# A two-block transformer on one core: 32x32 transposes and small transfers in place of 64 TensorE transposes, and four steps at new places

## The chip, the cores and the metric

One core of a Trainium2 chip runs the whole program. The metric is the device time of one execution in microseconds; lower is better. Before the change it is 789.58 us, the median of 3 runs (789.48 to 789.94). The core has TensorE (PE), VectorE (DVE), ScalarE (ACT), GpSimd (POOL) and SyncE (SP, which only issues transfers); each works through its own list in order, and semaphores tie the lists together.

## The reference, cut to what matters

One sequence of 256 positions and 1024 features goes through two blocks, all in float32.

```python
# first block
h = rmsnorm(x, norm1_g);  u = h @ w_in                       # 7168 columns: x_rnn g_rnn q k v g_br
ya = rg_lru(causal_dwconv(x_rnn)) * gelu(g_rnn)              # a linear recurrence over positions
q, k = rmsnorm per head(q, k)                                # 8 heads of 128
yb = causal softmax attention(q, k, v)                       # one block of 256 keys
x = x + (sig(g0) * (ya @ w_proj_rnn) + sig(g1) * (yb @ w_proj_attn)) @ w_out
h = rmsnorm(x);  x = x + (gelu(causal_dwconv(h @ w_up)) * (h @ w_gate)) @ w_down
# second block
h = rmsnorm(x);  proj = h @ w_in_2
o_a = windowed attention with sinks (8 heads of 64);  o_b = latent attention (8 heads, 64 + 32)
x = x + (sig(g_a) * (o_a @ w_o_swa) + sig(g_b) * (o_b @ w_o_mla)) @ w_out_2
h = rmsnorm(x);  x = x + (silu(h @ w_gate_2) * (h @ w_up_2)) @ w_down_2     # the last FFN
return rmsnorm(x, final_norm_g)
```

## The kernel before, in words

**Slabs.** All weights lie in HBM as 132 slabs of 128 x 2048 float32 (1 MB), in the order of their use (`slab_plan`, L47). SyncE loads slab s into one of three buffers `raw` as soon as VectorE is done with slab s - 3 (`load`, L476). ScalarE rounds it to a high part `whi` (L547), VectorE subtracts to get the low part `wlo` (L1010, `pre(s)`), and TensorE adds up three products for each pair of tiles (high by high, high by low, low by high; L1630, L1633, L1634, or L1677 and L1679). Activations are split in the same way. ScalarE may overwrite `whi` of slab s - 3 only when TensorE is done with it.

**Order.** Every engine's list is written out over the same slab numbers. The numbers that matter here: q, k and v are slabs 9 to 20, the gates of the first block 21 to 28 (`S_GATE` = 21), the two branch products 29 to 36, `w_out` 37 to 40, the first FFN 41 to 73, the second block up to 98, the last FFN 99 to 131. The FFNs are loops of three slabs a pass on each engine.

**Attention of the first block** (`att(step)` on ScalarE L574, VectorE L1057, TensorE L1721). One head enters at each slab from 21 on, and its stages lie one slab apart: at step u TensorE turns q and k of head u against an identity matrix (four transposes, L1731) and ScalarE copies them out of PSUM (L581, L582); at step u + 1 come the scores (L1742, L1743) and VectorE's mask and maximum; at u + 2 ScalarE's exponential; at u + 3 VectorE's normalisation (L1061 to L1063); at u + 4 TensorE turns the three tiles of probabilities (L1751) and ScalarE copies them to `pT` (L588); at u + 5 TensorE multiplies by the values (L1759, L1761) and both parts of the result are made (L592, L1075). The branch product from slab 33 on waits for these parts, head by head. Where q and k come from: ScalarE evacuates their slabs to `q_s` and `k_s` with positions on the partitions; VectorE scales k in the slab-18 turn of its list (L1235), which TensorE's first transposes wait for.

**The row sums.** TensorE sums squares of x for the first normalisation (`sums(0)`, L1707) between two chunks k of slab 2 (`hook` at L1950, before chunk 4), then ScalarE takes a root (L572) and VectorE the reciprocal.

**Second block.** Pairs of heads go through a similar pipeline (`PAIR_*`, L216 to L220; `pair_hi`, `pair_lo`, `pair_norm`). `pair_values` puts pairs p and p + 1 in one PSUM bank; `pair_lo` and `pair_norm` are called in that order in VectorE's list (L1480). `turned_lo` and `pre` of slab 96 (L1516) come at the start of `w_out`.

**The last FFN** (`ffn`, on SP L489, ACT L810, DVE L1321, PE L2045). In pass j TensorE makes the up and gate products of tile j + 1 and then the down product of tile j. The down product adds up in four PSUM banks over all passes. Ahead of the first one, `turned()` (L2049) puts the residual X, turned by sixteen transposes, into those banks. VectorE's `post(j)` sums and scales the products and makes the low parts of the next slabs between its steps.

```python
# L2098, TensorE in the first pass
if first and which == 2:
    e.wait_ge(rms_root, ROOTS[n])
    turned()
down(j - 1, s + 2, (base + 4) % RING, first=first and which == 1)
```

Of the kernel before, what the change touches and what calls it, by code (L numbers as in the profile page):

```python
# [16 lines left out]
P = 128  # L17
SEQ = 256
# [189 lines left out]
LAG_S, LAG_E, LAG_N, LAG_PT, LAG_PV = 1, 2, 3, 4, 5  # L208
# [40 lines left out]
def program(nc, t):  # L249
    f32, f32r = mybir.dt.float32, mybir.dt.float32r  # L250
    ALU, ACT, AX = mybir.AluOpType, mybir.ActivationFunctionType, mybir.AxisListType.X
    with ExitStack() as ctx:
# [71 lines left out]

        rnn_t = pr[:, :, :].rearrange("p a n -> p (a n)")[:, 0:4 * SEQ].rearrange("p (a n) -> p a n", a=4)
# [32 lines left out]
        PST, PSS, PSPT, PSPV, PSA, PSB = ps[2], (ps[3], ps[7]), (ps[4], ps[6]), ps[5], ps[6], ps[7]  # L358
# [28 lines left out]
        pair_pT = pT, VV[:, 1280:2048].rearrange("p (u n) -> p u n", u=2)  # L387
        PSX = (ps[0], ps[1], ps[2], ps[3])
# [27 lines left out]
        qk_ss, qk_scaled, v_ready = sem("qk_ss"), sem("qk_scaled"), sem("v_ready")  # L416
        aT, aTe, aS, aM, aE, aN, aPT, aPTe, aPV, aH, aL = (sem(n) for n in (
# [55 lines left out]
        def _(sp_eng):  # L473
# [14 lines left out]

            def ffn(base, then=None):  # L489
# [23 lines left out]
            for s in range(2 * RING, FFN1):  # L513
                load(s)
            ffn(FFN1)
# [17 lines left out]
        def _(e):  # L533
# [40 lines left out]
            def att(step):  # L574
                u = unit_of(step)
                if u is not None:
                    b = u % 2
                    e.wait_ge(aT, u + 1)
                    if u >= 2:
                        e.wait_ge(aS, u - 1)  # L580
                    e.activation(qT[:, b, :], PST[:, 0:SEQ], ACT.Copy)  # L581
                    e.activation(kT[:, b, :], PST[:, SEQ:2 * SEQ], ACT.Copy, scale=qkg[:, :]).then_inc(aTe, 1)  # L582
                u = unit_of(step - LAG_PT)
                if u is not None:
                    e.wait_ge(aPT, u + 1)
                    if u >= 2:
                        e.wait_ge(aPV, u - 1)
                    e.activation(pT[:, u % 2, :], PSPT[u % 2][:, 0:3 * P], ACT.Copy).then_inc(aPTe, 1)  # L588
# [5 lines left out]
                if u is not None:  # L594
                    e.wait_ge(aM, u + 1)
                    if u >= 3:
                        e.wait_ge(aPT, u - 2)
# [6 lines left out]
            def pair_turned(p):  # L604

                e.wait_ge(aT, pair(p))
# [22 lines left out]
            def pair_probs(p):  # L629

                e.wait_ge(aPT, pair(p))
# [3 lines left out]
            def pair_hi(p):  # L635

                e.wait_ge(aPV, pair(p + 1))
                e.activation(pairs[2][0][:, p:p + 2, :], PSPV2[p], ACT.Copy).then_inc(aH, 2)
# [360 lines left out]
        def _(e):  # L999
# [16 lines left out]

            def bc2(ap, n):
# [1224 lines left out]
```

## Time and profile before

| what | value |
|---|---|
| median of 3 runs | 789.58 us (789.48 to 789.94) |
| the profiled execution, its own time | 789.17 us |
| its span, first to last instruction | 787.4 us |
| instructions | 11265 |
| VectorE busy | 591.8 us (75%) |
| ScalarE busy | 452.6 us (57%) |
| moved by DMA | 141.08 MB, mean 179 GB/s |
| granted TensorE clock over the span | 0.999 of full speed |

A row of the timeline gives the start (us from the span's start), the duration of a group of like instructions, the engine, the line of the kernel, the operation, what it writes and reads, the shape, the count, and in brackets how long the engine was idle before it and on whose work. Matmuls overlap: a duration on PE reaches beyond the start of the next one, so the distance of two starts is what an instruction takes of the engine's time. A float32 product of the attention shows as two instructions (x2 where the source has one). "SPq" is SyncE issuing a transfer, not the transfer itself.

### The profile page before, as it was taken

The numbers are of one execution on the slowest core, as the hardware profiler recorded it, in microseconds if no ns is written. First come the engines' busy times: TensorE is split into PE (matmuls) and PEld (weight loads), VectorE is DVE, ScalarE is ACT, GpSimd is POOL, SyncE is SP. The second block draws the span as 40 slices with busy tenths as digits, with TensorE's granted clock in tenths as the row PEclk, the third lists the DMA queues.
The fourth block names the chain that finished last, engine by engine and source line by source line (L and its number), as shares of the span: only waits on it lengthen the run. The fifth ranks groups of instructions, "written<-read, shape, count | busy, mean of one in ns | idle before, by whom it ended". The sixth has DMA issues, their size and how long they took to land.

```text
span 787.4 us, 11265 instructions
## 1 busy us (share of the span) xinstructions
PE 780.1 (99%) x4246; PEld 669.1 (85%) x4246; DVE 591.8 (75%) x727; ACT 452.6 (57%) x591; POOL 44.3 (6%) x63
## 2 busy tenths in 40 slices
PE   9999999999999999999999999999999999999997
PEld 9998888888888888888888897888788888888886
DVE  6986897566578998778887867777789666666664
ACT  7679765666345654544444758765556535454444
POOL 0220231000000000000000031220000000000000
PEclk9999999999999999999999999999999999999999
DMA  8745555443545455465454352544445645454521
GB/s 329 246 171 198 193 185 214 158 160 122 199 161 199 148 207 196 171 209 205 167 206 160 144 219 106 173 163 159 161 143 206 214 163 210 161 212 171 202 107 53
DMA packets 22100, 141.08 MB, mean 179 GB/s; under 512 B 3410, under 2 KB 3762, under 8 KB 6066
## 3 DMA queue, kind: packets, MB, share of 16 engines
q1 hardware_dynamic: 21682, 140.13, 49.5%
q10 hardware_dynamic: 384, 0.49, 0.2%
q8 instruction: 22, 0.36, 0.2%
q14 instruction: 12, 0.10, 0.0%
HBM read 139.33 MB, written 1.05 MB: 178 GB/s over the span
## 4 chain that ended last, share of the span: by engine, by line
PE 96%; ACT 1%; DMA 1%; DVE 1%; issue 0%; SPq 0%
PE pp L1677 24%; PE pp L1630 18%; PE pp L1634 18%; PE pp L1633 18%; PE pp L1679 12%; PE pp L1819 1%; DMA first<-in_first 1%; PE pp L1851 1%; PE pp L1831 1%; PE pp L1894 0%; PE pp L1731 0%; PE pp L1743 0%; PE pp L1759 0%; ACT whi L657 0%; PE pp L1751 0%
## 5 line engine op out<-in xcount | busy, mean ns | idle before, releaser
L1010 DVE TENSOR_TENSOR wlo<-raw,whi 128x2048 fp32r<-128x2048 f32 x129 | 296.3, 2298 | 82.6 <-ACT whi L547 82.2
L547 ACT ACTIVATE whi<-raw 128x2048 fp32r<-128x2048 f32 x129 | 246.4, 1911 | 99.1 <-PE pp L1634 82.3
L1677 PE MATMUL pp<-ahilo,whi 128*128 128x512 f32 x832 | 261.9, 396 | 0.1
L1679 PEld LDWEIGHTS pp<-ahilo,wlo 128*128 128x128 f32 x832 | 156.3, 188 | 36.7
L1679 PE MATMUL pp<-ahilo,wlo 128*128 128x256 f32 x832 | 163.5, 278 | 0.0
L1630 PE MATMUL pp<-whi,ahilo 128*128 128x512 f32 (+1 forms) x336 | 133.1, 396 | 0.6 <-ACT first L778 0.6
L1634 PE MATMUL pp<-whi,ahilo 128*128 128x512 f32 (+1 forms) x336 | 130.5, 388 | 0.0
L1633 PE MATMUL pp<-wlo,ahilo 128*128 128x512 f32 (+1 forms) x336 | 130.3, 388 | 0.0
L1677 PEld LDWEIGHTS pp<-ahilo,whi 128*128 128x128 f32 x832 | 128.3, 189 | 2.0 <-DVE wlo L1010 0.3
L817 ACT ACTIVATE qk<-pp 128x512 f32<-128x512 f32 x44 | 26.3, 598 | 118.4 <-PE pp L1679 118.4
L1630 PE MATMUL pp<-whi,ahi 128*128 128x512 f32 (+1 forms) x218 | 85.0, 390 | 0.0
L1633 PE MATMUL pp<-wlo,ahi 128*128 128x512 f32 (+1 forms) x218 | 84.3, 387 | 0.0
L1634 PE MATMUL pp<-whi,alo 128*128 128x512 f32 (+1 forms) x218 | 84.3, 387 | 0.0
L1630 PEld LDWEIGHTS pp<-whi,ahilo 128*128 128x128 f32 x336 | 63.1, 188 | 13.7 <-issue 1.3
L1634 PEld LDWEIGHTS pp<-whi,ahilo 128*128 128x128 f32 x336 | 63.1, 188 | 12.9
L1633 PEld LDWEIGHTS pp<-wlo,ahilo 128*128 128x128 f32 x336 | 63.2, 188 | 11.7
L1333 DVE TENSOR_TENSOR qk<-pp,qk 128x512 f32<-128x512 f32 x44 | 30.3, 689 | 36.9 <-ACT qk L817 36.8
L1634 PEld LDWEIGHTS pp<-whi,alo 128*128 128x128 f32 x218 | 40.9, 188 | 8.5
L1630 PEld LDWEIGHTS pp<-whi,ahi 128*128 128x128 f32 x218 | 40.9, 188 | 7.6 <-issue 0.2
L1633 PEld LDWEIGHTS pp<-wlo,ahi 128*128 128x128 f32 x218 | 41.0, 188 | 7.3
L1630 PE MATMUL pp<-ahilo,whi 128*128 128x256 f32 x96 | 27.5, 286 | 0.0
L1633 PE MATMUL pp<-ahilo,whi 128*128 128x256 f32 x96 | 27.2, 283 | 0.0
(258 smaller groups left out, 823.9 us busy)
## 6 DMA issues: line engine op xcount, KB each, us to landing
raw<-in_slabs SPq DMA_DIRECT2D x125, 1024.0 KB, 4.8
raw<-in_slabs SPq DMA_DIRECT2D x2, 832.0 KB, 4.3
first<-in_first SPq DMA_DIRECT2D x2, 768.0 KB, 7.6
first<-in_first SPq DMA_DIRECT2D x3, 384.0 KB, 4.6
raw<-in_slabs SPq DMA_DIRECT2D x2, 512.0 KB, 10.0
raw<-in_slabs SPq DMA_DIRECT2D x1, 768.0 KB, 4.0
out<-gg SPq DMA_DIRECT2D x3, 256.0 KB, 2.1
xa<-in_final_norm_g SPq DMA_DIRECT2D x1, 512.0 KB, 7.3
```

What stands on the lines that cost most here:

```text
L547: e.activation(whi[slot][:, :], raw[slot][:, :], ACT.Copy).then_inc(hi_ready, 1)
L817: e.activation(dst, banks[:, :, SEQ:2 * SEQ], ACT.Copy).then_inc(f_cross, 1)
L1010: e.tensor_tensor(wlo[slot][:, :], raw[slot][:, :], whi[slot][:, :].bitcast(f32), ALU.subtract).then_inc(lo_ready, 1)
L1333: return e.tensor_tensor(dst, banks[:, :, 0:SEQ], dst, ALU.add)
L1630: e.matmul(out, lhs[0], rhs[0], start=first, stop=False, skip_group_check=True)
L1633: e.matmul(out, lhs[0], rhs[1], start=False, stop=False, skip_group_check=True)
L1634: return e.matmul(out, lhs[1], rhs[0], start=False, stop=last, skip_group_check=True)
L1677: e.matmul(out[:, m, :], w[m][0], act[:, k, :], start=k == 0, stop=False, skip_group_check=True)
L1679: ins = e.matmul(out[:, m, 0:SEQ], w[m][1], act[:, k, 0:SEQ], start=False, stop=k == KD - 1, skip_group_check=True)
L1819: ins = e.matmul(PSS2[:, i, cols], q[:, mine], k[:, keys], start=True, stop=True)
L1831: ins = e.transpose(PSPT2[:, o:o + P], soft[p % 2][:, i, P * j:P * j + P], ident[:, :])
L1851: ins = e.matmul(out[64 * i:64 * i + 64, mine], v, pair_pT[p % 2][:, i, keys], start=(p, h) == (p0, 0), stop=h == 1, skip_group_check=True)
```

## The change

Sixteen 32x32 squares make up a tile of 128x128. VectorE's `transpose` turns each square in its place of the 32 partitions; sixteen transfers from SBUF to SBUF then bring the rows of squares to their partitions (partitions 32a to 32a + 31 to 32b to 32b + 31).

- q and k of heads 2 to 7: VectorE turns the squares of q (`turn_heads(0)`, ahead of the sinks in the slab-18 turn) and of k (`turn_heads(1)`, after its scaling); SyncE issues 32 transfers after the load of slab 24; ScalarE copies from SBUF. Heads 0 and 1 keep their transposes.
- probabilities of all eight heads: VectorE turns the squares after the normalisation; SyncE issues 16 transfers for a head into `pT`, ahead of the loads of slabs 29 to 36; ScalarE's copy goes away.
- the last residual: VectorE turns X in two halves in the first two passes of the last FFN (the second is written out of the loop), SyncE moves each with 16 transfers, and VectorE adds them to the four banks after the first down product.
- moved: `sums(0)` to before chunk 5; `pair_norm` ahead of `pair_lo`; head pair 7 into a bank of its own with its two halves evacuated one by one; the low part of slab 96 in two halves, the first one earlier.

```diff
 # names
+        FAR = HEADS - 2
+        heads_in = XA[:, 0:2 * FAR * P], GG[:, 0:2 * FAR * P]
+        heads_far = tuple(x[:, :, 2 * P:].rearrange("p h (i u n) -> p h i u n", i=4, u=FAR) for x in (q_s, k_s))
+        probs_in = [XA[:, 3 * P * i:3 * P * i + 3 * P] for i in range(2)]
+        probs_far = [pT[:, i, :].rearrange("p (i t n) -> p t i n", i=4, t=3) for i in range(2)]
+        rows_in, rows_turned = GG, VV
+        PSPVL = ps[5][:, 0:SEQ]
 # SyncE
+            def move_heads(i):
+                e.wait_ge(head_squares32[i], 1)
...
+                for a in range(4):
+                    for b in range(4):
+                        e.dma_start(dst[P // 4 * b:P // 4 * b + P // 4, a],
+                                    src[P // 4 * a:P // 4 * a + P // 4, b]).then_inc(head_turned[i], 16)
+            def move_probs(u):
+                e.wait_ge(aN, u + 1)
+                if u >= 2:
+                    e.wait_ge(aPV, u - 1)
+                for a in range(4):
+                    for b in range(4):
+                        e.dma_start(pT[P // 4 * b:P // 4 * b + P // 4, u % 2, 96 * a:96 * a + 96],
+                                    probs_in[u % 2][P // 4 * a:P // 4 * a + P // 4, 96 * b:96 * b + 96]).then_inc(
+                                        probs_turned[u % 2], 16)
+            def move_rows(c):
+                e.wait_ge(row_squares32, c + 1)
...
+                        e.dma_start(dst[P // 4 * b:P // 4 * b + P // 4, a, :, 4 * c:4 * c + 4, :],
+                                    src[P // 4 * a:P // 4 * a + P // 4, b, :, 4 * c:4 * c + 4, :]).then_inc(
+                                        row_turned[c], 16)
                 if then:
                     then()
-                with e.Fori(1, STEPS) as j:
+                    for s in range(base + 2, base + 8):
+                        load(s)
+                        if s >= base + 6:
+                            move_rows(s - base - 6)
+                with e.Fori(3 if then else 1, STEPS) as j:
             for s in range(2 * RING, FFN1):
+                if unit_of(s - S_GATE - LAG_N - 5) is not None:
+                    move_probs(s - S_GATE - LAG_N - 5)
                 load(s)
+                if s == S_GATE + 3:
+                    move_heads(0)
+                    move_heads(1)
 # ScalarE, att(step)
+                    if u < 2:
+                        e.wait_ge(aT, u + 1)
+                        q_from, k_from = PST[:, 0:SEQ], PST[:, SEQ:2 * SEQ]
+                    else:
+                        e.wait_ge(head_turned[0], 16 * 16)
+                        e.wait_ge(head_turned[1], 16 * 16)
                         e.wait_ge(aS, u - 1)
...
-                u = unit_of(step - LAG_PT)
-                if u is not None:
-                    e.wait_ge(aPT, u + 1)
...
-                    e.activation(pT[:, u % 2, :], PSPT[u % 2][:, 0:3 * P], ACT.Copy).then_inc(aPTe, 1)
             def pair_hi(p):
+                for i in range(2):
+                    e.activation(pairs[2][0][:, p + i, :], (PSPV2[p][:, 0, :], PSPVL)[i], ACT.Copy).then_inc(aH, 1)
 # VectorE, att(step)
+                    if un >= 2:
+                        e.wait_ge(probs_turned[un % 2], 16 * 16 * (un // 2))
+                    e.transpose(probs_in[un % 2].rearrange("p (j t n) -> p t j n", j=4, t=3),
+                                pr[:, un % 3, :].rearrange("p (t j n) -> p t j n", t=3, j=4)).then_inc(aN, 1)
+            def turn_heads(i):
+                if i == 0:
+                    e.wait_ge(bank_free["act"], emptied(GROUP_OF[(S_K - 1, 0)])[1])
+                for h in range(HALVES):
+                    ins = e.transpose(in_squares(heads_in[i], FAR)[:, h],
+                                      (q_s, k_s)[i][:, h, 2 * P:].rearrange("p (u j n) -> p u j n", u=FAR, j=4))
+                ins.then_inc(head_squares32[i], 1)
                 if s == S_V + 1:
+                    turn_heads(0)
                     e.wait_ge(sink_T, 1)
...
                     ins.then_inc(qk_scaled, 1)
+                    e.wait_ge(qk_scaled, 1)
+                    turn_heads(1)
+                def turn_rows(c):
+                    e.transpose(in_squares(rows_in[:, :], KD)[:, :, 4 * c:4 * c + 4].rearrange("p h u j n -> p u h j n"),
+                                X[:, 4 * c:4 * c + 4, :].rearrange("p u (h j n) -> p u h j n", h=HALVES, j=4)).then_inc(
+                                    row_squares32, 1)
+                def add_turned():
+                    e.wait_ge(down_used, STEPS)
+                    for c in range(2):
+                        e.wait_ge(row_turned[c], 16 * 16)
+                        for h in range(HALVES):
...
+                            e.tensor_tensor(bank, bank, turned_rows[:, h, 4 * c:4 * c + 4], ALU.add).then_inc(
+                                row_added, 1)
-                post(0, lambda: pre(base + 3), lambda: pre(base + 4), lambda: None)
-                with e.Fori(1, STEPS - 1) as j:
+                post(0, lambda: pre(base + 3), lambda: pre(base + 4), (lambda: turn_rows(0)) if which == 2 else lambda: None)
+                if which == 2:
+                    post(1, lambda: (pre(base + 5), turn_rows(1)), lambda: pre(base + 6),
+                         lambda: (add_turned(), pre(base + 7)))
+                with e.Fori(which, STEPS - 1) as j:
 # VectorE, second block
+                if normal is not None:
+                    pair_norm(normal)
                 if values is not None:
                     pair_lo(values)
-                if normal is not None:
-                    pair_norm(normal)
                         if s == S2_OUT - 1 and h == 0:
                             for i in range(2):
                                 turned_lo(4 + i)
+                            lo_half(S2_OUT + 1, 0)
                 if s == S2_OUT:
                     for i in range(2):
                         turned_lo(6 + i)
-                    pre(s + 1)
+                    lo_half(s + 1, 1)
 # TensorE
-                if u is not None:
+                if u is not None and u < 2:
...
-                    for i in range(3):
-                        ins = e.transpose(PSPT[u % 2][:, P * i:P * i + P], pr[:, u % 3, P * i:P * i + P], ident[:, :])
...
-                    e.wait_ge(aPTe, u + 1)
+                    e.wait_ge(probs_turned[u % 2], 16 * 16 * (u // 2 + 1))
...
-                    e.matmul(PSPV[:, 0:SEQ], v[0], pT[:, u % 2, 0:SEQ], start=True, stop=False,
+                    e.matmul(PSPV[:, 0:SEQ], v[0], probs_far[u % 2][:, 0:2], start=True, stop=False,
...
-                    out = PSPV2[p0][:, p - p0, :]
+                    out = PSPVL if p == 7 else PSPV2[p0][:, p - p0, :]
...
-                        if hook and (i, k) == (0, 4):
+                        if hook and (i, k) == (0, 5 if s == S_XR + 2 else 4):
...
-                def turned():
...
+                    if which == 2:
+                        if first:
+                            e.wait_ge(rms_root, ROOTS[n])
+                        else:
+                            e.wait_ge(row_added, 4)
+                    down(j - 1, s + 2, (base + 4) % RING, first=first)
```

## Rows read from the trace of the kernel before

**Rows 1.** The page's table of busy time: engine, busy us, share, instructions.
```profile
PE 780.1 (99%) x4246; PEld 669.1 (85%) x4246; DVE 591.8 (75%) x727; ACT 452.6 (57%) x591; POOL 44.3 (6%) x63
```

**Rows 2.** The page's chain that ended last, shares of the span.
```profile
PE 96%; ACT 1%; DMA 1%; DVE 1%; issue 0%; SPq 0%
```

**Rows 3.** Timeline of PE at steps of the attention in slabs 22, 26, 27.
```profile
131.04 0.60 PE L1731 MATMUL pp<-ident,qk 128*128 128x128 f32 x4
...
157.70 0.60 PE L1731 MATMUL pp<-ident,qk 128*128 128x128 f32 x4
158.13 0.28 PE L1742 MATMUL pp<-qkT 128*128 128x128 f32 x1
...
165.27 0.60 PE L1731 MATMUL pp<-ident,qk 128*128 128x128 f32 x4
...
166.36 0.49 PE L1751 MATMUL pp<-ident,pr 128*128 128x128 f32 x3
166.69 0.60 PE L1759 MATMUL pp<-pT,vv 128*128 128x256 f32 x2
```

**Rows 4.** Timeline of PE at the residual's transposes in the last FFN.
```profile
620.14 1.91 PE L2054 MATMUL pp<-ident,first 128*128 128x128 f32 x16
621.80 0.47 PE L1630 MATMUL pp<-whi,ahi 128*128 128x512 f32 x1
```

**Rows 5.** Timeline of PE at the row sums, and of PEld at slab 96.
```profile
19.55 0.28 PE L1633 MATMUL pp<-ahilo,whi 128*128 128x256 f32 x1
19.66 0.28 PE L1634 MATMUL pp<-ahilo,wlo 128*128 128x256 f32 x1
20.13 0.48 PE L1718 MATMUL pp<-vv,ones 128*128 128x256 f32 x1 [0.19 <-DVE vv L1024]
...
580.57 0.19 PEld L1677 LDWEIGHTS pp<-ahilo,whi 128*128 128x128 f32 x1 [0.33 <-DVE wlo L1010]
```

**Rows 6.** Timeline of SP: a load after a wait, then small transfers behind it.
```profile
18.05 0.33 SPq L481 DMA_DIRECT2D raw<-in_slabs  x1
18.42 0.43 SPq L507 DMA_DIRECT2D ident<-in_ident  x1
...
20.36 0.54 SPq L510 DMA_DIRECT2D ropeA<-in_rope_a  x1
...
21.46 0.37 SPq L512 DMA_DIRECT2D rowt<-in_swa_sinks  x1
```

**Rows 7.** Timeline of ACT: the copy of the rotated key, SBUF to SBUF.
```profile
501.45 0.74 ACTq L619 DMA_DIRECT2D gg<-gg  x1
```

**Rows 8.** Timeline of DVE: low parts of slabs 21, 22, 25; a normalisation.
```profile
118.88 2.28 DVE L1010 TENSOR_TENSOR wlo<-raw,whi 128x2048 fp32r<-128x2048 f32 x1
...
124.53 2.28 DVE L1010 TENSOR_TENSOR wlo<-raw,whi 128x2048 fp32r<-128x2048 f32 x1
...
142.04 2.29 DVE L1010 TENSOR_TENSOR wlo<-raw,whi 128x2048 fp32r<-128x2048 f32 x1 [1.72 <-ACT whi L547]
...
144.65 0.35 DVE L1063 TENSOR_SCALAR pr<-pr,rinv 128x256 f32<-128x256 f32 x1
```

**Rows 9.** The page's DMA issues: count, KB each, median us from issue to landing.
```profile
raw<-in_slabs SPq DMA_DIRECT2D x125, 1024.0 KB, 4.8
...
out<-gg SPq DMA_DIRECT2D x3, 256.0 KB, 2.1
```

**Rows 10.** Timeline of ACT: the high part of slab 25.
```profile
140.10 1.91 ACT L547 ACTIVATE whi<-raw 128x2048 fp32r<-128x2048 f32 x1
```

**Rows 11.** Timeline of PE: the values of head 7.
```profile
206.93 0.59 PE L1759 MATMUL pp<-pT,vv 128*128 128x256 f32 x2
```

**Rows 12.** Timeline of DVE and PE in the last FFN's first passes.
```profile
613.84 0.68 DVE L1371 TENSOR_TENSOR qk<-qk 128x512 f32<-128x512 f32 x1
...
624.98 0.68 DVE L1371 TENSOR_TENSOR qk<-qk 128x512 f32<-128x512 f32 x1
...
638.51 0.40 PE L1630 MATMUL pp<-whi,ahi 128*128 128x512 f32 x1
```

More of the change, by code:

```diff
@@ L604, in pair_turned @@
             def pair_turned(p):
-                e.wait_ge(aT, pair(p))
+                e.wait_ge(aT, 2 + p + 1)
                 e.wait_ge(aS, pair(p) - 1)
@@ L1092, in pair_max @@
                 e.wait_ge(aS, pair(p))
-                e.wait_ge(aPT, pair(p) - 2)
+                if p >= 2:
+                    e.wait_ge(aPT, p - 1)
                 x = soft[p % 2][:, 0:2, :]
@@ L1107, in pair_lo @@
             def pair_lo(p):
-                e.wait_ge(aH, pair(p + 1))
-                e.tensor_tensor(pairs[2][1][:, p:p + 2, :], PSPV2[p], pairs[2][0][:, p:p + 2, :].bitcast(f32),
-                                ALU.subtract).then_inc(aL, 2)
+                if p < 6:
+                    e.wait_ge(aH, pair(p + 1))
+                    e.tensor_tensor(pairs[2][1][:, p:p + 2, :], PSPV2[p], pairs[2][0][:, p:p + 2, :].bitcast(f32),
+                                    ALU.subtract).then_inc(aL, 2)
+                    return
+                for i in range(2):
+                    e.wait_ge(aH, pair(p + i))
+                    e.tensor_tensor(pairs[2][1][:, p + i, :], (PSPV2[p][:, 0, :], PSPVL)[i], pairs[2][0][:, p + i, :].bitcast(f32),
+                                    ALU.subtract).then_inc(aL, 1)
             e.memset(epst[:, :], EPS)
@@ L1824, in pair_turn_probs @@
                 e.wait_ge(aN, pair(p))
-                e.wait_ge(aPTe, pair(p) - 1)
+                if p:
+                    e.wait_ge(aPTe, p)
                 if p == 0:
@@ L1834, in pair_values @@
             def pair_values(p0):
-                e.wait_ge(aPTe, pair(p0 + 1))
+                e.wait_ge(aPTe, p0 + 2)
                 if p0 == 0:
@@ L1851, in pair_values @@
                             ins = e.matmul(out[64 * i:64 * i + 64, mine], v, pair_pT[p % 2][:, i, keys],
-                                           start=(p, h) == (p0, 0), stop=h == 1, skip_group_check=True)
+                                           start=h == 0 and p in (p0, 7), stop=h == 1, skip_group_check=True)
                     ins.then_inc(aPV, 1)
@@ L2048, in ffn @@
                 free0 = emptied(g_up)[1]
-                def turned():
-                    for c in range(KD):
-                        e.wait_ge(*x_value(n, c))
-                        for h in range(HALVES):
-                            e.matmul(ps[2 + 2 * h + c // 4][:, P * (c % 4):P * (c % 4) + P],
-                                     X[:, c, P * h:P * h + P], ident[:, :], start=(c % 4 == 0), stop=False,
-                                     is_transpose=True, skip_group_check=True)
                 def wide(j, s, slot, i, free, ready=always):
@@ L2097, in step @@
                              lambda: e.wait_ge(bank_free["dve"], (j - 1) * 2 + (free0 + i)))
-                    if first and which == 2:
-                        e.wait_ge(rms_root, ROOTS[n])
-                        turned()
-                    down(j - 1, s + 2, (base + 4) % RING, first=first and which == 1)
+                    if which == 2:
[4 more added lines that the diff above has]
+                    down(j - 1, s + 2, (base + 4) % RING, first=first)
                 step(1, True)
```

58 lines of the change are left out of this document (38 added, 20 removed).

## The prediction

> **What bounds it now.** I read the page's busy table first: TensorE is busy 99% of the span [rows 1]. That table counts matmuls that overlap, so the chain of waits must say whether TensorE waits: 96% of what ends last is its own work [rows 2]. What leaves TensorE is then worth its pitch there, start to start, if nothing else ends later. So the pitch comes third, from TensorE's timeline in the first block's attention [rows 3]: four transposes of q and k from 157.70 to the next matmul at 158.13, 0.43 us (0.11 each; the row itself shows 0.60, since its end overlaps the next), and three of the probabilities from 166.36 to 166.69, 0.33 us. The step repeats after 7.57 us (157.70 to 165.27). The sixteen transposes of the last residual stand in one piece, 620.14 to 621.80, 1.66 us [rows 4].
>
> The sum below is made against the profiled execution, 789.17 us (span 787.4 and 1.8 around it). The median of the runs is 0.41 above it, which is added at the end. A measurement of this kernel can tell about 0.2% (1.6 us) from no change.
>
> **What TensorE loses.** Heads 2 to 7 lose their four transposes: 6 x 0.43 = 2.6 us. All eight heads lose the three of the probabilities: 8 x 0.33 = 2.6. The residual's sixteen: 1.7. Together 6.9 us, all of it time in which TensorE waits for nothing.
>
> **The four moved steps.** (a) The row sums move from the fifth chunk of slab 2 to the sixth. Matmuls there follow each other after 0.11 to 0.12 us (19.55, 19.66), so the one at 20.13 comes 0.35 late [rows 5]; the six matmuls of a chunk now fill that gap. ScalarE's root comes 0.4 later, and VectorE, which waits for it, is in a 2.3 us subtraction then; 0.3 gained. (b) The low part of slab 96 in two halves: TensorE waits 0.33 for it at 580.57 [rows 5]. The first half, 1.1 us, now stands ahead of the last quarters of the branch, which the merge's transposes wait for; between nothing and 0.3, I take 0.2. (c) The normalisation ahead of the low part and (d) head pair 7 in a bank of its own with halves of its evacuation change which of two short operations comes first, and something waits for each; bounds -0.2 to 0.3, I take 0.1. Together 0.6, so the gain is 7.5 us, and 781.7 is the time if all that is added is hidden.
>
> **What is added to SyncE's queue.** SyncE so far issues one load a slab. It gets 32 transfers for q and k behind the load of slab 24, 16 for each of eight heads ahead of the loads of slabs 29 to 36, and 16 twice in the last FFN: 192. The trace has few issues back to back [rows 6]: after a wait one takes 0.33 us, and the next starts 0.37 after it (18.05 to 18.42), so 0.04 lie between; in the train the plain one takes 0.43 (18.42), 0.47 with that gap, one of small pieces 0.54 (20.36), and the one with a single piece 0.37 (21.46), 0.41 with the gap. No row has a transfer from SBUF to SBUF of 32 partitions on SyncE; the only one at all is ScalarE's copy of the rotated key, 0.74 [rows 7]. So an issue costs between 0.37 and 0.74. I take 0.41 for the probabilities (32 pieces of 384 bytes, nearer to the row with one piece than to those with 128) and 0.44 for q, k and the residual (64 pieces, half way to 0.47).
>
> What that does on the path, in the order of the queue. VectorE is done with slab 21 at 121.16 [rows 8]. Its transposes I price by its subtraction of 2048 columns in 2.28 us, 1.1 ns a column: 0.88 for 768 columns, 0.45 for 384, 1.15 for 1024 (bounds: half and twice that). So q's squares are there at 122.9, and the 32 issues end at 122.9 + 32 x 0.44 = 137.0; k's squares come at 128.1, before their turn. The load of slab 25 is issued behind them, lands 4.8 later [rows 9], ScalarE's part takes 1.9 [rows 10] and VectorE's 2.3: 146.0, where it was 144.3 [rows 8]. TensorE takes that slab only at about 151 (slab 22 at 131.04, slab 26 at 157.70 [rows 3]). But VectorE treats the first head's probabilities behind it: 0.7 for the normalisation (144.33 to 145.00) and 0.45 for the transpose, 147.2. From there SyncE is never idle: 8 x 16 x 0.41 = 52.5, seven loads between them at 0.41 = 2.9, and 2.1 until the last has landed (as the output's [rows 9]): 204.7. TensorE would begin the values of head 7 at 206.93 - 5.2 = 201.7 [rows 11]. It waits 3.0 us. A head costs the queue 17 x 0.41 = 7.0 us and TensorE at most 7.57 - 0.76 = 6.8, so earlier heads wait less, and their waits are within this one. In general the wait is 160 x (issue - 0.397), the issue averaged over the 160 that stand ahead; below that nothing waits.
>
> Behind the new waits: SyncE's loads follow the transfers of a head, but have two slabs of lead. VectorE, from head 2 on, turns a head only when the transfers two heads back have landed; behind that are the next maximum and the next low part. TensorE waits for the same transfers for its values, so this adds nothing.
>
> **The rest.** VectorE's turn of q and k delays slab 22's low part from 126.8 to 130.3 [rows 8]; TensorE takes the slab at 131.04: hidden, with 0.7 to spare. ScalarE loses the eight evacuations of the probabilities and copies q and k from SBUF instead of PSUM: nothing, it waits for TensorE. In the last FFN the first half of the rows is turned behind VectorE's product, 614.5 + 1.15 = 615.7 [rows 12]. SyncE issues 16 at 0.44, a load, 16 more: 630.1, landed 632.2. VectorE would be ready for its four additions at 625.7, does two, and waits for the second half; behind that wait stand two additions at 0.7, the low part of slab 106 (2.3) and the step's own (0.7): 636.6. TensorE wants them at 638.51 - 1.7 = 636.8. Hidden, just; each 0.01 more an issue costs 0.3 there. The passes written out of two loops are the same instructions: nothing.
>
> Sum: 789.17 - 7.5 + 3.0 = 784.7, with 0.41 for the median **785.1**.
>
> **Rivals.** *All is hidden.* An issue costs what follows a lone load, 0.37 a start [rows 6]: no wait, 781.7 + 0.4 = 782.1. Against it stands every later row of the train, all at 0.41 or more. The Trainium skill, "DMA: Bandwidth & Descriptors", section "Issuing engines are not separate DMA queues", calls the sequencer's time to initiate a DMA usually small beside the DMA itself. By that rule this rival holds; the trace disagrees for 16 of them, some 7 us of issuing beside 2.1 of landing.
>
> *SyncE's queue is the bound, and the kernel slower.* The issue costs what the plain rows of 128 partitions show, 0.47, whatever its size. Then the wait is 160 x 0.073 = 11.7 us in the attention, and 0.8 in the FFN: 781.7 + 12.5 + 0.4 = 794.6. It decides from 0.44 on, where the wait has eaten the gain. For it: even a single piece takes 0.37, so most of an issue doesn't depend on size. Against it: that piece is still cheaper by 0.06. The same page's section "Rules for kernel authors" wants many small transfers coalesced, since under 64 KB one pays mostly overhead; the transfers here have 12 to 48 KB, and no run here shows the threshold.
>
> *Three dimensions are dear.* If q, k and the residual cost what ScalarE's copy did, 0.74 [rows 7], the heads' 32 end 9.6 us later, and the residual's 32 cost 9.4: 785.1 + 19.0 = about 804.
>
> *VectorE's turn takes twice its price.* Slab 22 then waits 2.8 us, much of which the wait for head 7 would have taken anyway: about 787.
>
> **How the numbers follow.** Forecast, issues of 0.40 to 0.43, 782.5 to 788: 0.27. All hidden: 0.19. VectorE at half pace: 0.05. An issue of 0.43 to 0.45, within 0.2%: 0.13. SyncE's queue as the bound: 0.28. Three dimensions dear: 0.08. So faster 0.51, same 0.13, slower 0.36. Both signs hold much, since 0.01 us an issue is 1.6 us of time. The forecast's own range is 782.5 to 788; the one given reaches from the hidden case, less 1 us, to 796, which takes in most of the queue's case; the dear case and the queue's dearer end are left out.
>
> **What would show it.** On SyncE's timeline the pitch of 16 transfers into pT: under 0.40 gives the hidden case, 0.47 the slow one. TensorE's waits should name pT's transfers, longest at the last heads; if there are none, the queue was not the bound. VectorE's new lines should take 0.45, 0.9 and 1.15 us; the transposes of q and k beyond head 1, of the first block's probabilities and of X must be gone from TensorE's lines. I am wrong if slab 22, 25 or 106 makes TensorE wait, or if time is lost where nothing was changed, which would mean loads that collide.

## The result: 5.5% slower, and the profile after

832.57 us, the median of 4 runs (832.23 to 833.09), against 789.61 for the kernel before (4 runs, 789.48 to 789.94): a ratio of 1.0545 (95% interval 1.0533 to 1.0558), 43 us slower. 785.1 was forecast, and the range ended at 796. The profiled execution took 832.66, its span is 830.9 (787.4 before).

The page of the changed kernel: busy time, the chain that ended last by engine and by line, and DMA issues (median us from issue to landing).

```profile
PE 790.2 (95%) x4182; PEld 673.2 (81%) x4182; DVE 603.5 (73%) x747; ACT 449.2 (54%) x584; POOL 44.3 (5%) x63
...
PE 74%; SPq 9%; DVE 7%; ACT 4%; issue 3%; DMA 1%; DVEq 0%; ACTq 0%
...
pT<-xa SPq DMA_DIRECT2D x128, 12.0 KB, 1.8
```

TensorE has 64 instructions less than in [rows 1], and yet 10 us more of busy time; of the chain it now holds 74%, where it held 96% [rows 2]. The largest new share, 9%, is SPq's: SyncE issuing transfers (VectorE, ScalarE and "issue" have 12% more between them). The transfers themselves land 1.8 us after their issue.

SyncE's timeline (start, duration of the group, line, what it writes and reads, count), at the lines L498 (loads of slabs), L513 (q and k) and L523 (probabilities):

```profile
120.89 0.33 SPq L498 DMA_DIRECT2D raw<-in_slabs  x1
122.64 10.34 SPq L513 DMA_DIRECT2D qk<-xa  x16
133.02 10.21 SPq L513 DMA_DIRECT2D qk<-gg  x16
143.28 9.71 SPq L498 DMA_DIRECT2D raw<-in_slabs  x4
153.93 10.38 SPq L523 DMA_DIRECT2D pT<-xa  x16
164.35 0.58 SPq L498 DMA_DIRECT2D raw<-in_slabs  x1
164.99 10.01 SPq L523 DMA_DIRECT2D pT<-xa  x16
175.04 0.58 SPq L498 DMA_DIRECT2D raw<-in_slabs  x1
```

In these rows sixteen transfers take 10.0 to 10.4 us. From start to start one takes (143.28 - 122.64) / 32 = 0.645 us for q and k, and for a head's probabilities (175.04 - 164.99) / 16 = 0.628. The forecast had 0.44 and 0.41. A head with its load comes every 175.04 - 164.35 = 10.69 us, where TensorE needs at most 6.8: from 153.93 until the last head's train ends at 240.2 SyncE hardly idles and TensorE follows it. Even the load in the train takes 0.58, and 0.33 after a wait.

TensorE's timeline at the values of heads 4 and 7, and at the second down product of the last FFN (L1868 is the first product of the values, L1759 before; the bracket is the idle time ahead of the row and what ended it):

```profile
203.99 0.39 PE L1751 MATMUL pp<-whi,alo 128*128 128x512 f32 x1
208.80 0.67 PE L1868 MATMUL pp<-pT,vv 128*128 128x256 f32 x2 [4.42 <-issue]
...
209.99 0.63 PE L1750 MATMUL pp<-wlo,ahi 128*128 128x512 f32 x1
210.41 0.63 PE L1751 MATMUL pp<-whi,alo 128*128 128x512 f32 x1
...
241.46 1.19 PE L1868 MATMUL pp<-pT,vv 128*128 128x256 f32 x2 [3.37 <-issue]
...
246.72 0.55 PE L1747 MATMUL pp<-whi,ahilo 128*128 128x512 f32 x1
247.10 0.39 PE L1750 MATMUL pp<-wlo,ahilo 128*128 128x512 f32 x1
...
680.07 0.80 PE L1747 MATMUL pp<-whi,ahi 128*128 128x512 f32 x1 [6.61 <-DVE alo L1471]
```

Two things stand here. The values of head 7 start at 241.46, where they started at 206.93 [rows 11]. And behind the waits a matmul of 512 columns takes 0.42 us start to start (209.99 to 210.41) instead of 0.23. The windows of the same stretch (start and end, span, busy us of each engine with counts, granted clock, DMA share, GB/s) say why:

```profile
208.00:247.00 39.00, 29.34 (x98) 23.12 (x99) 15.32 (x17) 9.90 (x12) 0.00 (x0) 0.78 0.44 149
241.46:247.10 5.64, 5.64 (x14) 4.54 (x15) 1.46 (x2) 0.38 (x1) 0.00 (x0) 0.51 0.96 373
247.00:260.00 13.00, 13.00 (x62) 10.83 (x62) 6.92 (x6) 4.73 (x4) 0.00 (x0) 1.00 0.42 165
```

The granted clock averages 0.78 up to 247, is 0.51 from 241.46 to 247.10, and 1.00 from there: behind the wait of 3.37 us TensorE runs for a while at the lower of its two levels (1.2 of 2.4 GHz), and the matmuls at 0.42 show the same behind the wait of 4.42. That is why it shows more busy time than before. Of SyncE's delay, the waits proper are only a part; slow matmuls fill the rest.

In the last FFN the residual's second half is late. VectorE's timeline (L1301, L1140 and L1479 are its 32x32 transposes; L1491 adds the turned residual to the banks):

```profile
120.78 1.83 DVE L1301 STREAM_TRANSPOSE xa<-qk 128x768 f32<-128x768 f32 x2
...
153.33 0.58 DVE L1140 STREAM_TRANSPOSE xa<-pr 128x384 f32<-128x384 f32 x1
...
651.00 1.24 DVE L1479 STREAM_TRANSPOSE gg<-first 128x1024 f32<-128x1024 f32 x1
...
663.90 1.30 DVE L1491 TENSOR_TENSOR pp<-pp,vv 128x512 f32<-128x512 f32 x2 [1.67 <-DMA vv<-gg]
675.92 1.30 DVE L1491 TENSOR_TENSOR pp<-pp,vv 128x512 f32<-128x512 f32 x2 [10.72 <-DMA vv<-gg]
```

VectorE, in order, waits 10.72 us for the second half's transfers, and the low parts behind it wait too. The prediction had named this as a sign of being wrong: slab 106, whose low part stands there, makes TensorE wait. The second half's own train was slower than the others, 11.40 / 16 = 0.71 us an issue, and no run says why:

```profile
663.18 11.40 SPq L534 DMA_DIRECT2D vv<-gg  x16
```

TensorE's waits (line, what it waited for, us in total, times, longest) show both places, L1868 in the attention and L1747 in the last FFN:

```profile
PE pp L1868 <- issue: 13.3, 4, 4.4
PE pp L1868 <- DMA pT<-xa: 10.2, 4, 3.7
PE pp L1747 <- DVE alo L1471: 6.6, 1, 6.6
PE pp L1859 <- issue: 1.9, 1, 1.9
```

The 43.5 us of the span by three points: the values of head 7 come 34.5 later (206.93 to 241.46). The second down product of the last FFN, at 638.51 before [rows 12], starts at 680.07, 41.6 later; so 7.0 are added between. The terms known come to 6.9: 2.7 of slow matmuls up to 247.10 and the wait of 6.6, less 1.7 of transposes and 0.7 that the moved steps give back. The last 1.9 are slow matmuls behind that wait.

### The profile page after: what moved, and what is told of

It is laid out like the page before. It is cut to its first block, busy times and chain, and to the rows that moved or that the text cites. A ratio compares the mean times of both kernels' runs of the same rounds, so it can differ in the third digit from the quotient of the medians.

```text
span 830.9 us, 11304 instructions
## 1 busy us (share of the span) xinstructions
PE 790.2 (95%) x4182; PEld 673.2 (81%) x4182; DVE 603.5 (73%) x747; ACT 449.2 (54%) x584; POOL 44.3 (5%) x63
## 4 chain that ended last, share of the span: by engine, by line
PE 74%; SPq 9%; DVE 7%; ACT 4%; issue 3%; DMA 1%; DVEq 0%; ACTq 0%
PE pp L1794 21%; PE pp L1747 12%; PE pp L1750 12%; PE pp L1751 12%; PE pp L1796 11%; SPq L523 4%; DVE wlo L1073 4%; SPq L534 2%; SPq L513 2%; ACT whi L605 1%; PE pp L1928 1%; PE pp L1961 1%; PE pp L1941 1%; DMA raw<-in_slabs 1%; DVE pr L1293 1%
## 5 line engine op out<-in xcount | busy, mean ns | idle before, releaser
L1747 PE MATMUL pp<-whi,ahilo 128*128 128x512 f32 (+1 forms) x336 | 135.9, 404 | 1.6 <-ACT first L841 1.6
L1751 PE MATMUL pp<-whi,ahilo 128*128 128x512 f32 (+1 forms) x336 | 132.7, 395 | 0.0
L1750 PE MATMUL pp<-wlo,ahilo 128*128 128x512 f32 (+1 forms) x336 | 132.6, 395 | 0.0
L1747 PE MATMUL pp<-whi,ahi 128*128 128x512 f32 (+1 forms) x218 | 87.5, 401 | 6.6 <-DVE alo L1471 6.6
L1750 PE MATMUL pp<-wlo,ahi 128*128 128x512 f32 (+1 forms) x218 | 86.5, 397 | 0.0
L1747 PEld LDWEIGHTS pp<-whi,ahilo 128*128 128x128 f32 x336 | 64.9, 193 | 15.2 <-issue 1.4
L1751 PEld LDWEIGHTS pp<-whi,ahilo 128*128 128x128 f32 x336 | 64.5, 192 | 13.6
L1747 PEld LDWEIGHTS pp<-whi,ahi 128*128 128x128 f32 x218 | 42.5, 195 | 15.0 <-DVE alo L1471 6.8
L1868 PE MATMUL pp<-pT,vv 128*128 128x256 f32 x16 | 7.9, 591 | 23.5 <-issue 13.3
L651 ACT ACTIVATE ahilo<-pp 128x256 fp32r<-128x256 f32 x8 | 3.1, 383 | 47.3 <-PE pp L1870 47.3
```

The lines of the kernel that those rows point to most:

```text
L1747: e.matmul(out, lhs[0], rhs[0], start=first, stop=False, skip_group_check=True)
L1750: e.matmul(out, lhs[0], rhs[1], start=False, stop=False, skip_group_check=True)
L1751: return e.matmul(out, lhs[1], rhs[0], start=False, stop=last, skip_group_check=True)
```

## The experiments

Ten kernels ran. The theory was that one thing costs: the issue of a transfer in SyncE's queue, at 0.63 us. What had to be told apart was why it costs that, whether the queue is all of it, and what the low clock adds.

**What an issue costs.** Trains of 16 (six or eight where the transfers are large) behind the last output of the kernel before; the diff shows the kinds.

```diff
+            Q = P // 4
+            a, b = raw[0], raw[1]
...
+            trains = [
+                [(a[Q * (i % 4):Q * (i % 4) + Q, cols[i]], b[Q * (i // 4):Q * (i // 4) + Q, cols[i]]) for i in range(16)],
+                [(a[:, cols[i]], b[:, cols[i]]) for i in range(16)],
+                [(a[Q * (i % 4):Q * (i % 4) + Q, cols[i]], slab[Q * (i % 4):Q * (i % 4) + Q, cols[i]]) for i in range(16)],
+                [(a[:, cols[i]], slab[:, cols[i]]) for i in range(16)],
...
+                [((a, raw[2])[i // 4][Q * (i % 4):Q * (i % 4) + Q, :], b[Q * ((i + 1) % 4):Q * ((i + 1) % 4) + Q, :]) for i in range(8)],
+                [(a[i:i + 1, cols[0]], b[i:i + 1, cols[0]]) for i in range(16)],
+                [(scratch[i], b[:, 0:384]) for i in range(6)],
...
```

> The kernel before, with nine trains of transfers back to back behind its last output, each train awaited before the next one starts: on SyncE 16 x SBUF to SBUF of 32 partitions x 384 bytes from one group of 32 partitions to another (as the probabilities'), 16 x SBUF to SBUF of 128 x 384 bytes on the same partitions, 16 x HBM to SBUF of 32 x 384 bytes, 16 x HBM to SBUF of 128 x 384 bytes, 6 x HBM to SBUF of 128 x 8 KB (a slab), 8 x SBUF to SBUF of 32 x 8 KB, 16 x SBUF to SBUF of one partition x 384 bytes, 6 x SBUF to HBM of 128 x 1.5 KB, 16 x the first kind again; then 16 of the first kind from ScalarE's queue, and 16 from GpSimd's. Theory 'kind': what made the issue 0.63 us instead of the 0.41 forecast is that both ends lie in SBUF; then all SBUF-to-SBUF trains start every 0.59 to 0.65 us whatever their partitions and bytes, the HBM trains every 0.40 to 0.47. Theory 'partitions': it is the piece of 32 partitions; then the 32-partition trains take 0.63 from HBM too, and SBUF to SBUF on 128 partitions 0.40 to 0.47. Theory 'size': it is the bytes; then 32 x 8 KB takes far more than 32 x 384 bytes, and one partition far less. From ScalarE the same price as from SyncE within 0.05; GpSimd's is open.

One execution was taken. The timelines of SyncE, train by train, and of ScalarE and GpSimd. In order: SBUF to SBUF of 32 partitions, of 128; HBM to SBUF of 32, of 128; SBUF to SBUF of 32 x 8 KB, and of one partition; SBUF to HBM; and the first kind from ScalarE's and from GpSimd's queue.

```profile
787.33 10.10 SPq L551 DMA_DIRECT2D raw<-raw  x16
798.60 10.18 SPq L551 DMA_DIRECT2D raw<-raw  x16
810.06 7.31 SPq L551 DMA_DIRECT2D raw<-in_slabs  x16
818.70 7.47 SPq L551 DMA_DIRECT2D raw<-in_slabs  x16
...
845.15 6.75 SPq L551 DMA_DIRECT2D raw<-raw  x8
856.58 10.25 SPq L551 DMA_DIRECT2D raw<-raw  x16
867.99 2.81 SPq L551 DMA_DIRECT2D scratch<-raw  x6
...
883.83 10.19 ACTq L1031 DMA_DIRECT2D raw<-raw  x16
...
895.80 8.07 POOL L1666 DMA_DIRECT2D raw<-raw  x16 [379.64 <-DMA raw<-raw]
```

Theory "kind" holds for transfers of up to 48 KB, the largest that the change has. With both ends in SBUF such a transfer takes 10.1 / 16 = 0.63 us of the queue, whether it has 32 partitions, 128 or one single piece of 384 bytes. With one end in HBM it takes 0.46 to 0.47, written or read. "Partitions" falls: 32 partitions from HBM take 7.31 / 16 = 0.46. "Size" falls in that range: one partition inside SBUF takes 10.25 / 16 = 0.64. Beyond it the theory was too strong: pieces of 32 x 8 KB (256 KB) take 6.75 / 8 = 0.84. ScalarE's queue costs the same as SyncE's, GpSimd's 8.07 / 16 = 0.50.

**The same transfers from HBM.** The number, the shapes and the waits stay; what changes is the price of an issue, and the probabilities' transfers land 2.5 us after it, not 1.8.

```diff
-                                    probs_in[u % 2][P // 4 * a:P // 4 * a + P // 4, 96 * b:96 * b + 96]).then_inc(
+                                    t["slabs"][5][P // 4 * a:P // 4 * a + P // 4, 96 * b:96 * b + 96]).then_inc(
```

(and so for q, k and the residual)

> The changed kernel with the sources of its 192 transfers in HBM, the same shapes and bytes from a slab of weights: it leaves out that the turned values reach q, k, the probabilities and the residual. Theory 'price': only the source sets the issue's 0.634; at 0.464 the attention's waits are 160 x (0.464 - 0.397) = 10.7 us, the last FFN's 0.6, 1 to 2 more at the low clock: 781.5 + 12 to 13 = 794, the time of the rival with the 0.47 of the loads. Rival 'number': an issue among other transfers of this kind costs 0.63 whatever its source: 832.

795.4 us (794.07 to 796.42), a ratio of 1.0079 (1.0064 to 1.0095). This is about the time of the prediction's second rival, 794.6, which was priced with 0.47; here the 32 of q and k take 0.47 each, and the trains of the probabilities with their loads 0.48 on the average. SyncE's and TensorE's timelines:

```profile
147.87 7.79 SPq L523 DMA_DIRECT2D pT<-in_slabs  x16
155.70 0.42 SPq L498 DMA_DIRECT2D raw<-in_slabs  x1
...
214.23 0.67 PE L1868 MATMUL pp<-pT,vv 128*128 128x256 f32 x2 [2.58 <-issue]
```

The rival put head 7's values at 201.7 + 11.7 = 213.4; they start at 214.23, a wait of 12.5 where it had 11.7. Its 0.8 in the last FFN is missing: TensorE waits for no transfer there. That the sum comes out within 0.8 is in part luck, since these two misses cancel; the wait itself was right to 7%. So the law of the queue (the issues that stand ahead times their price, then the landing) was right, and the 37 us between 795.4 and 832.6 are what the source in SBUF costs.

**One part at a time.** Three versions of the changed kernel, each with parts undone, and the moved steps alone.

```diff
 # without the residual's part: sixteen transposes on TensorE again
-                    down(j - 1, s + 2, (base + 4) % RING, first=first)
+                    if first and which == 2:
+                        e.wait_ge(rms_root, ROOTS[n])
+                        turned()
+                    down(j - 1, s + 2, (base + 4) % RING, first=first and which == 1)
 # without q and k: no turn_heads, no move_heads
-                if u is not None and u < 2:
+                if u is not None:
 # without the probabilities: no move_probs, three transposes and ScalarE's copy
-                    e.wait_ge(probs_turned[u % 2], 16 * 16 * (u // 2 + 1))
+                    e.wait_ge(aPTe, u + 1)
```

> Only the four moved steps, all TensorE transposes kept. Theory: the moves do what the trace of the changed kernel shows, 0.28 us before slab 21 and 0.72 between the two FFNs, and nothing else: 788.6 (789.6 - 1.0). Rival: the 0.72 came from the shifted phase behind the attention, not from the moves: 789.3. A third: moving the low part is what delays something: above 789.6.

788.38 us, 0.9987 (0.9978 to 0.9996): 1.0 us (interval 0.3 to 1.7), as the theory said. The second explanation, 0.3, lies at the edge of the interval, but the trace speaks against it: head 7's values start at 206.36 where they started at 206.93, and the last product of the last FFN's row sums starts at 601.9 where it started at 603.2. So some 0.7 is gained between the two, with the attention unchanged.

> The changed kernel with the residual's part undone (sixteen transposes on TensorE again, no second half to wait for). Theory 'queue': the last FFN's loss is the 6.6 us wait behind the second half's 16 issues plus some 1.8 us of matmuls at the low clock behind it, less the 1.66 us of transposes: 832.6 - 6.7 = 825.9, and the wait at the first down product's successor is gone. Rival 'attention only': the wait in the last FFN takes the place of another one there, and the time stays above 830.

826.31 us (825.79 to 827.23): 6.3 less than the whole change, and the wait at L1747 is gone.

> The changed kernel with the probabilities' and the residual's parts undone: q and k of heads 2 to 7 by 32 transfers, and the moved steps. Theory 'queue': the 32 issues at 0.64 us hold back the load of slab 25 until 143.3 us, TensorE waits 1.9 + 0.8 + 1.0 us between 143 and 155 as in the changed kernel and runs about 1.6 us longer at the low clock behind that; it has 2.6 us of transposes and 1.0 of moved steps less: 789.6 + 3.7 + 1.6 - 3.6 = 791.3. Rival 'crowd': these waits are there only because the probabilities' transfers follow; alone the part gains its 2.6 and the moves 1.0: 786.0.

790.09 us, 1.001 (1.0001 to 1.002). 1.7 above the moves alone, where 2.6 less were to be had: this part alone costs 4.3 at 0.64 an issue. 1.9 of that is a wait and some 1.6 are slow matmuls behind it (until 149.86); the other 0.8 is not accounted for, and is no more than the spread of the two versions. The theory's first wait is there, its second and third are not; they needed the probabilities' train. What TensorE waits for, 1.9 us at 143.6, is not the load of slab 25, as this expectation had it, but ScalarE, whose timeline shows it idle until the last piece of k:

```profile
145.00 0.42 ACT L640 ACTIVATE qkT<-qk 128x256 f32<-128x256 f32 x1 [6.43 <-DMA qk<-gg]
```

> The changed kernel with the parts of q and k and of the residual undone: the 128 transfers of the probabilities on SyncE, and the moved steps. Theory 'queue': the train starts when the first head is turned, at 145.5 instead of 153.9, and ends 128 x 0.634 + 7 x 0.6 + 1.8 later, at 232.7, where TensorE (four transposes a head again) would want it at 204.3; 28.4 us of waits and 2.8 at the low clock behind the last, less 1.0 and 2.6: 789.4 - 3.6 + 31.2 = 817.0. Rival 'parts': each part has its own price, whatever stands ahead of it in the queue; then it is what the version without the residual's part and the one with q and k alone leave for it: 788.4 + 826.3 - 790.1 = 824.6.

816.65 us (816.03 to 817.4), 0.35 from the forecast by the queue and 8 from the one by parts. The train starts at 145.34, and head 7's values at 233.52. What a part costs depends on where its train starts.

**The low clock by itself.** Products that nothing reads fill the waits of heads 3 to 7.

```diff
+                    for i in range(5 if u >= 3 else 0):
+                        e.matmul(ps[(4, 6)[u % 2]][:, 0:3 * P], ident[:, :], masks[:, 0, :], start=True, stop=True)
                     e.wait_ge(probs_turned[u % 2], 16 * 16 * (u // 2 + 1))
```

> The changed kernel with five more products of 384 columns (0.64 us each) on TensorE ahead of its wait for the probabilities of heads 3 to 7, into a bank that nothing reads: 3.2 us of work a head more, in a wait of 1.4 to 4.4. Theory 'idle': TensorE's matmuls at 0.427 us behind each wait are the price of having waited; kept busy it stays at 0.227 us, and as the queue sets when the last probabilities land, only what follows them is shorter: 832.6 - 2.8 = 829.8. Rival 'no clock': the slow matmuls have nothing to do with the idling: 832.6, or later by what the added work delays.

830.06 us (829.47 to 831.12), 2.5 less than the changed kernel, with 16 us more work on TensorE. Its timeline at head 7, and the window that stood at 0.78:

```profile
236.64 3.39 PE L1865 MATMUL pp<-masks,ident 128*128 128x384 f32 x10
241.33 0.70 PE L1870 MATMUL pp<-pT,vv 128*128 128x256 f32 x2 [1.31 <-DMA pT<-xa]
...
242.56 0.40 PE L1751 MATMUL pp<-whi,ahilo 128*128 128x512 f32 x1
242.79 0.39 PE L1747 MATMUL pp<-whi,ahilo 128*128 128x512 f32 x1
```

```profile
208.00:247.00 39.00, 35.58 (x145) 26.05 (x144) 15.31 (x17) 9.92 (x12) 0.00 (x0) 1.00 0.43 150
```

The values start when they did (241.33 for 241.46), since SyncE sets that, and the matmuls behind them follow at 0.23 instead of 0.42. So in this kernel the idling brings the low clock, and only its part behind the last wait is lost time; ahead of that it eats into time that would have been waited.

**Other queues.** The same 192 transfers, first split between SyncE and GpSimd, which has no other work in these stages from 122.5 on; then all on GpSimd.

```diff
 # GpSimd, behind its last part of the recurrence
+            move_heads(e, 1)
+            for u in range(HEADS):
+                move_probs(e, u, (2, 3), probs_pool)
 # SyncE
-                    move_probs(s - S_GATE - LAG_N - 5)
+                    move_probs(e, s - S_GATE - LAG_N - 5, (0, 1), probs_turned)
```

> The changed kernel with its transfers on two queues: q's 16 on SyncE, k's 16 on GpSimd, and of every head's 16 and every half's 16 eight on each; the same 192 transfers. Theory 'queue': SyncE needs 8 x 0.634 + 0.5 = 5.6 us a head and GpSimd 8 x 0.489 = 3.9, TensorE 6.8, so no transfer is waited for; left are the gains: 1.0 of moved steps, 2.6 + 2.6 + 1.7 of transposes: 789.4 - 7.9 = 781.5. Rival 'transfers': their number or their landing is what costs (they share the DMA engines with the 1 MB loads); then the time stays within some us of 832. Rival 'VectorE': its added work or its in-order waits keep part of the loss: 785 to 790.

783.31 us (782.6 to 785.27), 0.9926 (0.9912 to 0.994): faster than before by 0.7%, so number and landing of the transfers are not what costs. The Trainium skill, "Perfetto Trace Analysis", section "DMA Optimizations", says that balancing transfers over SyncE, ScalarE and GpSimd may help where an issuing engine is full of DMA slices. The trace agrees: against the changed kernel it gave 49 us. The time missed the expectation by 1.8. TensorE's waits keep one:

```profile
PE pp L1865 <- issue: 1.4, 1, 1.4
```

It is ScalarE again, waiting for k until 144.4. GpSimd's last four pieces of k were issued from 134.8 on and landed a median of 7.1 us later, where a piece of q or k otherwise takes about 2. Two loads of slabs had been issued ahead of them, at 133.4 and 134.0; the last version below puts that to the test.

> All 192 transfers on GpSimd's queue, the loads alone on SyncE. Theory 'queue': the same law with another price. q's and k's 32 end at 122.6 + 32 x 0.489 = 138.3, before the first head's probabilities are there (145.5); the eighth head's have landed at 145.5 + 128 x 0.489 + 1.6 = 209.7, where TensorE would take them at 201.7: 8.0 us of waits, some 2 more at the low clock behind them, nothing in the last FFN: 781.5 + 8 + 2 = 791.5. Rival 'SyncE alone': it was the loads behind the transfers that cost; without them in the queue no wait is left: 781.5. Rival 'transfers': 825 or more.

807.94 us (807.25 to 808.49), 16.4 above the expectation. GpSimd's timeline, ScalarE's, TensorE's waits, and its timeline at the values of heads 6 and 7:

```profile
132.13 8.44 POOL L496 DMA_DIRECT2D qk<-gg  x16
```

```profile
146.13 0.42 ACT L641 ACTIVATE qkT<-qk 128x256 f32<-128x256 f32 x1 [7.38 <-DMA qk<-gg]
```

```profile
PE pp L1867 <- issue: 4.8, 1, 4.8
PE pp L1746 <- DVE alo L1466: 4.5, 1, 4.5
```

```profile
213.50 0.77 PE L1867 MATMUL pp<-pT,vv 128*128 128x256 f32 x1 [4.83 <-issue]
...
222.42 0.59 PE L1867 MATMUL pp<-pT,vv 128*128 128x256 f32 x2
```

Two terms of the expectation were off. q, k and the residual cost 8.44 / 16 = 0.53 on GpSimd, not 0.49, and k's last piece has landed only when ScalarE goes on at 146.1, so ScalarE is late and the train of the probabilities starts at 153.7 instead of 145.5: 8.2 us. In the last FFN the 32 pieces end late enough for a wait of 4.5, and some 1.7 of slow matmuls follow: 791.5 + 8.2 + 6.2 = 805.9, 2.0 short. Nor is the place of the wait the one expected: head 7's values start at 222.42 without a wait, and the last wait in the attention is head 6's, 4.83 us up to 213.50. The probabilities' transfers land 1.6 to 5.0 us after their issue here, not 1.6; that this is what held head 6 up is likely, but not shown. So the late start and the price are borne out here, the law up to head 7 is not. Rival "SyncE alone" falls: with nothing but loads on SyncE the kernel is still 18.6 us slower than before.

**A version that beats both.** From the 1.4 us left: q's and k's transfers are split as well, so that they are issued ahead of the loads.

```diff
-                    move_heads(e, 0)
+                    move_heads(e, 0, (0, 1), head_turned)
+                    move_heads(e, 1, (0, 1), head_turned)
 # GpSimd
-            move_heads(e, 1)
+            move_heads(e, 0, (2, 3), head_pool)
+            move_heads(e, 1, (2, 3), head_pool)
```

> As the version with two queues, but q's and k's 16 transfers too are split eight and eight. There ScalarE waits until 144.4 for k's last piece, which was issued at 136.4 behind two loads, and TensorE waits 1.4 us at 143.5 for ScalarE's copies. Theory 'order': split, k's pieces are issued by 128.2 + 8 x 0.634 = 133.3, ahead of the loads, and have landed at about 135.3, before ScalarE asks for them at 138.5; that wait and the late score behind it go: 783.3 - 1.6 = 781.7. Rival 'loads': the wait was that for slab 25, whose load stays behind the transfers: 783.3.

781.43 us (780.73 to 781.56) against 789.86 for the kernel before on the same chip: 0.9893 (0.9876 to 0.9909). Measured so, it is 1.1% faster than before. Its page, busy time and chain:

```profile
PE 772.8 (99%) x4182; PEld 663.6 (85%) x4182; DVE 603.0 (77%) x747; ACT 449.0 (58%) x584; POOL 92.8 (12%) x159
...
PE 99%; ACT 1%; DVE 0%; issue 0%
```

ScalarE copies head 2 at 138.55 without waiting, GpSimd's pieces of k land 2.1 us after their issue, and TensorE waits for no transfer. So the order of the issues was it.

## Why the prediction was wrong

**The step that failed** is the price of an issue: "I take 0.41 for the probabilities (32 pieces of 384 bytes, nearer to the row with one piece than to those with 128) and 0.44 for q, k and the residual". It measured 0.63 to 0.645 in most trains, and 0.71 for the residual's second half. The choice went by the size of the pieces, from rows of loads out of HBM [rows 6]; the size does not matter up to 48 KB, and that both ends lie in SBUF does. The one row of that kind, ScalarE's copy at 0.74 [rows 7], was taken for a matter of three dimensions and held for the dear case alone, and for only two of the three parts. Both ends, 0.37 and 0.74, did hold the price, but the range did not follow the upper one: 0.63 on all 192 was left out of it.

**The chain behind it was right where it leads to head 7.** With the measured prices it reads: q's squares at 122.6, 32 issues of 0.645 to 143.3, slab 25's load, high and low part and the first head's turn to 153.9, then 128 x 0.634 and seven loads of 0.64, 85.6, and 1.8 until the last has landed: 241.3. Measured: 241.46. The wait of 3.0 became a delay of 241.46 - 201.7 = 39.8. Of these, 27.2 are waits (23.5 at the values of all eight heads, the longest, 4.42, at head 4 and not at the last; 3.7 at three places ahead of them); the rest, some 13 by difference, goes to matmuls at the low clock in between. The last FFN, "hidden, just; each 0.01 more an issue costs 0.3", gives 0.2 x 30 = 6.0 for 0.64 instead of 0.44, less the 0.2 to spare: 5.8; 6.6 were measured, and the second half's dearer train, 16 x 0.07 = 1.1, more than fills that gap.

**TensorE's gain was right.** 6.9 of transposes and 0.6 of moved steps were forecast. The moves alone gave 1.0 (interval 0.3 to 1.7), and the version without waits gives 8.4 against before (7.2 to 9.8), so 7.4 for the transposes.

**The rivals.** The second one, SyncE's queue as the bound, is what happened, with its price set too low: at 0.47 to 0.48, transfers from HBM gave its time. "All is hidden" fell: an issue costs 0.63, not 0.37. The Trainium skill, "DMA: Bandwidth & Descriptors", section "Issuing engines are not separate DMA queues", calls the time to initiate a DMA usually small beside the DMA itself. The trace does not agree for these small ones: one issue takes 0.63 us of the 1.8 until its transfer has landed, and sixteen in a row 10.1. "VectorE at half pace" fell too: 0.92, 0.58 and 1.24 us for 768, 384 and 1024 columns, where 0.88, 0.45 and 1.15 were forecast.

**What was not foreseen.** First, the low clock behind the waits: 2.7 us behind the attention and 1.9 in the last FFN, 4.6 in all; no row of before shows TensorE idle for long, so nothing there could price it. Second, ScalarE: its copy of head 2 needs the last of the 32 pieces, and its high parts stand behind that copy. The prediction watched the load of slab 25 alone. By its own price k would have landed at 139, just when ScalarE asks; at 0.645 ScalarE stood idle for 6.42 us:

```profile
144.65 0.42 ACT L646 ACTIVATE qkT<-qk 128x256 f32<-128x256 f32 x1 [6.42 <-DMA qk<-gg]
```

Put together: 781.7 + 39.8 + 6.6 + 4.6 + 0.4 = 833.1, where 832.57 was measured.

## What to carry to other kernels

A small transfer is paid for by the engine that issues it: count the issues in each queue, multiply them by the price of their own kind (here, for up to 48 KB, 0.63 us from SBUF to SBUF, 0.46 with one end in HBM, about 0.5 on GpSimd), and compare the sum with the stage that is to hide it. Where no row shows an operation of the same kind, let the range reach to the nearest one, and don't pick a price by size between rows of another kind. If the queue is the bound, sharing the issues with an idle engine may be all that is missing: here that turned 5.5% slower into 1.1% faster, while all of them on the idle engine left 2.3% slower.

## What was unexpected of the hardware

- An issue from SBUF to SBUF takes 0.63 us of SyncE's queue, whether it moves 384 bytes or 48 KB (0.84 for 256 KB), and 0.46 to 0.47 if one end is in HBM. ScalarE's queue takes 0.64 for the same, GpSimd's 0.50 for pieces of 32 x 384 bytes and 0.53 for those of q, k and the residual.
- In a train a load, too, takes the longer time: 0.58 for a slab behind transfers inside SBUF, 0.42 behind transfers from HBM, 0.33 after a wait.
- Small transfers issued behind loads of 1 MB landed late: in the version with two queues 7.1 us after their issue, where they otherwise take about 2, although the loads stood in another engine's queue. Issued ahead of the loads they landed after 2.1.
- TensorE's granted clock fell to the lower level, 1.2 GHz, behind some waits and not behind others. It is 0.51 from 241.46 to 247.10, behind 3.37 us. Behind 1.94 us it is 1.00 in the changed kernel (145.57 to 152.00), behind 1.95 us 0.57 with q and k alone (145.90 to 149.90), and behind the 2.58 us at 214.23 of the version from HBM it stayed at 1.00 (214.00 to 220.00). What decides between them no run here shows. Filling the waits with work that nothing reads gave 2.5 us back.
